# Feed-forward of a two-layer diffusion backbone as one block in three chunks, with rounded down-projection products and a third raw weight slot in the scan

## The reference, cut to what matters

```python
def _conv_ffn(h, lp):
    u, g = jnp.split(h @ lp['ffn_up'], 2, axis=-1)          # 1024 -> 2 * 2816
    g = _dwconv3(g, lp['ffn_conv'], lp['ffn_conv_b'])       # three taps along the tokens
    return (jax.nn.gelu(g, approximate=False) * u) @ lp['ffn_down']   # 2816 -> 1024

# in each layer, after the token mixer; alpha = 4 ** 0.25
x = _layernorm(alpha * x + mod[2] * lat_mix, ln1_g[i], ln1_b[i])
x = _layernorm(alpha * x + mod[5] * _conv_ffn(_modulate(x, mod[3], mod[4]), lp), ln2_g[i], ln2_b[i])
```

## Time and profile before

| | us |
|---|---|
| median of 3 runs | 4132.44 |
| lowest and highest of them | 4118.54, 4132.5 |
| profiled execution, its own time | 4123.52 |
| its span, first to last instruction | 4121.7 |
| TensorE busy in it | 3571.3 (87%) |
| VectorE, ScalarE, GpSimd busy | 1515.8, 997.4, 1047.9 |
| mean granted TensorE clock | 0.942 |

### The profile page before, as it was taken

The page is one execution under the profiler, slowest core; times in us unless marked ns, Lnnn a source line. Parts: engine busy times, 40 slices in busy tenths (PEclk is TensorE's granted clock), DMA queues, the critical chain, the costliest instruction groups (busy, mean ns, idle before and its releaser), DMA issues. The chain is left out here.

```text
span 4121.7 us, 80895 instructions
## 1 busy us (share of the span) xinstructions
PE 3571.3 (87%) x36124; PEld 2659.2 (65%) x36124; DVE 1515.8 (37%) x2207; ACT 997.4 (24%) x1690; POOL 1047.9 (25%) x641
## 2 busy tenths in 40 slices
PE   5979989999787777999899597998889877679987
PEld 4658878888556553888644376877778554448843
DVE  3243434432676244311101524454442663342112
ACT  3312212221464120322100141222121552213200
POOL 2122233333014011322100322243444022224401
PEclk9989999999999889999999798999999999889998
DMA  6653344343214141122243143344443222413321
GB/s 243 205 156 101 105 127 119 91 122 100 93 51 150 69 138 40 57 67 62 94 147 133 51 160 121 94 116 117 132 130 105 100 92 93 163 41 97 87 102 41
DMA packets 454724, 444.30 MB, mean 108 GB/s; under 512 B 19876, under 2 KB 373338, under 8 KB 447466
## 3 DMA queue, kind: packets, MB, share of 16 engines
q1 hardware_dynamic: 452794, 430.35, 33.3%
q10 hardware_dynamic: 1584, 8.78, 0.6%
HBM read 350.32 MB, written 88.74 MB: 107 GB/s over the span
## 5 line engine op out<-in xcount | busy, mean ns | idle before, releaser
L855 PE MATMUL ps<-I-280_h_hi,I-1958_w_hi 128*128 128x256 f32 (+1 forms) x832 | 302.1, 363 | 32.5 <-POOL I-1959_w_lo L329 32.5
L855 PE MATMUL ps<-I-281_h_lo,I-1958_w_hi 128*128 128x256 f32 (+1 forms) x832 | 285.7, 343 | 4.0 <-issue 4.0
L855 PE MATMUL ps<-I-280_h_hi,I-1959_w_lo 128*128 128x256 f32 (+1 forms) x832 | 285.7, 343 | 0.0
L855 PE MATMUL ps<-I-22095_h_hi,I-23492_w_hi 128*128 128x512 f32 (+1 forms) x544 | 216.8, 398 | 32.5 <-POOL I-23493_w_lo L329 30.5
L2074 PE MATMUL ps<-I-21346_w_down,I-18202_hf 128*128 128x512 f32 x528 | 234.1, 600 | 9.1 <-DMA I-21346_w_down<-in_ffn_down 9.1
L855 PE MATMUL ps<-I-22095_h_hi,I-23493_w_lo 128*128 128x512 f32 (+1 forms) x544 | 203.6, 374 | 0.3 <-issue 0.3
L855 PE MATMUL ps<-I-22096_h_lo,I-23492_w_hi 128*128 128x512 f32 (+1 forms) x544 | 203.6, 374 | 0.0
L855 PEld LDWEIGHTS ps<-I-280_h_hi,I-1958_w_hi 128*128 128x128 f32 x832 | 159.3, 192 | 55.5 <-POOL I-1959_w_lo L329 33.7
L2074 PEld LDWEIGHTS ps<-I-21346_w_down,I-18202_hf 128*128 128x128 f32 x528 | 99.2, 191 | 143.3 <-issue 133.3
L338 PE MATMUL ps<-I-18203_h_hi,I-18207_w_hi 128*128 128x512 f32 x704 | 179.7, 336 | 1.1 <-DVE I-18204_h_lo L380 1.1
L338 PE MATMUL ps<-I-18204_h_lo,I-18207_w_hi 128*128 128x512 f32 x704 | 179.5, 336 | 0.0
(11 more groups left out here) (824 smaller groups left out, 8169.3 us busy)
## 6 DMA issues: line engine op xcount, KB each, us to landing
I-1957_w_raw<-in_w_in SPq DMA_DIRECT2D x52, 512.0 KB, 4.7
I-23491_w_raw<-in_w_in SPq DMA_DIRECT2D x52, 512.0 KB, 5.0
I-21350_ada_w<-in_ada_w SPq DMA_DIRECT2D x24, 1024.0 KB, 4.9
I-18206_w_raw<-in_ffn_up SPq DMA_DIRECT2D x44, 512.0 KB, 3.9
I-37126_w_raw<-in_ffn_up SPq DMA_DIRECT2D x44, 512.0 KB, 3.9
proj_d<-I-1960_result SPq DMA_DIRECT2D x52, 384.0 KB, 2.8
I-482_ada_w<-in_ada_w SPq DMA_DIRECT2D x16, 1024.0 KB, 5.7
I-21346_w_down<-in_ffn_down SPq DMA_DIRECT2D x22, 512.0 KB, 5.9
```

The costliest lines, as they stand in the source:

```text
L855: m = pe.matmul(bank(6 + i % 2, n_c), w[:, k, :], hv[:, k, c0:c0 + n_c], start=k == 0 and v == 0, stop=k == KT - 1 and v == 2)
```

## The change

In `rwkv_scan`, the raw ring has three slots, so that the weights of slot s+3 are loaded where those of slot s+2 were. Results go to a DRAM tensor `pair_d` with 272 rows per tile; a q or k tile is stored twice in it, and the swapped copy is fetched in four DMAs of 32 rows instead of eight of 16. `reset` is one tile for both directions, and the swapped copy lands in `ada_row`. `ffn` and `ffn_down` become one `ffn` with one stage: the 22 inner tiles are worked in chunks of 8, 8 and 6, first the up slots of a chunk and then its down slots for either half of the columns. The down weights come through the same rings as the up weights, and the inner tile is split too (`hp`: ScalarE `hf_hi`, GpSimd `hf_lo`), so that down products are three rounded ones. Each of the six passes (chunk, half) ends in VectorE multiplying by the gate row and adding to x. The gate rows are made after up slots 2 and 5, the `ada_w` steps stand behind every second slot from slot 8 on, the final norm goes tile by tile with the normalization on ScalarE, and the output is written by four DMAs, one per tile.

```diff
-            rings = weight_rings(s2, 2, 2)
+            rings = weight_rings(s2, 3, 2)
...
-                        for at_p, from_p in swap:
-                            sp.dma_start(rs[at_p:at_p + 16, :], src[from_p:from_p + 16, 0:SEQ]).then_inc(sem("swap_in"), 16)
+                        for u in range(4):
+                            sp.dma_start(rs[32 * u:32 * u + 32, :], swapped(slots[s][0])[u]).then_inc(sem("swap_in"), 16)
...
-                        if s + 2 < len(slots):
-                            load(s + 2)
+                        if s + 3 < len(slots):
+                            load(s + 3)
...
                         sp.dma_start(proj_d[j, :, 0:w], res[:, s % 2, 0:w]).then_inc(sem(f"stored{s % 2}"), 16)
+                        if s in turned:
+                            sp.dma_start(pair_d[j, TWIN + 16:TWIN + 16 + P, 0:SEQ], res[:, s % 2, 0:SEQ]).then_inc(sem(f"stored{s % 2}"), 16)
...
+        def ffn(l, h, last):
...
+            CH = 8
+            chunks = [range(j, min(j + CH, FT)) for j in range(0, FT, CH)]
...
+            n_pairs = 4 if last else 3
...
+            ada_at = {8 + 2 * e: e for e in range(len(ada))}
...
+                hp = [sb(s2, f"hf_{i}", [P, CH, n_tok], F32R) for i in ("hi", "lo")]
...
+                            pe.wait_ge(sem("hf_lo"), j + 2)
+                            for t in range(nt):
+                                if opens(g) and t % 2 == 0:
+                                    released(first_user[g] + t // 2)
+                                for k in range(2):
+                                    for v, (hv, w) in enumerate(((0, whi), (0, wlo), (1, whi))):
+                                        m = pe.matmul(pt_of(a, t), hp[hv][:, k0 + k, t * P:(t + 1) * P], wide(w)[:, k, :],
+                                                      start=k0 + k == 0 and v == 0, stop=k0 + k == n_k - 1 and v == 2)
...
+                            act.wait_ge(sem("hf"), j + 1)
+                            act.activation(hp[0][:, j % CH, :], cv[:, j % 2, 0:n_tok], ACT.Copy).then_inc(sem("hf_hi"), 1)
...
+                            pool.wait_ge(sem("hf_hi"), j + 1)
+                            pool.tensor_tensor(hp[1][:, j % CH, :], cv[:, j % 2, 0:n_tok], hp[0][:, j % CH, :].bitcast(F32),
+                                               ALU.subtract).then_inc(sem("hf_lo"), 1)
...
+                        dve.tensor_tensor(part[:, i % 2, :], pt_of(cn, t), gate[:, t // LT, c], ALU.mult).then_inc(sem("z1"), 1)
+                        dve.wait_ge(sem("z1"), i + 1)
+                        if cn[0] == 0:
+                            dve.scalar_tensor_tensor(x[:, t, c], x[:, t, c], ALPHA, part[:, i % 2, :], ALU.mult, ALU.add).then_inc(sem("z2"), 1)
+                        else:
+                            dve.wait_ge(sem("z2"), i + 1 - 2 * nt)
+                            dve.tensor_tensor(x[:, t, c], x[:, t, c], part[:, i % 2, :], ALU.add).then_inc(sem("z2"), 1)
+                        if cn[0] == LC:
+                            dve.wait_ge(sem("z2"), i + 1)
+                            dve.bn_stats(st[:, t, cn[1], :], x[:, t, c]).then_inc(sem("st"), 1)
...
-        def ffn_down(l, hf, last):
...
-                                for t in range(nt):
-                                    if n and g == 0:
-                                        pe.wait_ge(sem("z1"), t + 1)
-                                    for k in range(KG):
-                                        m = pe.matmul(bank(t), hf[:, g * KG + k, t * P:(t + 1) * P], ring[:, i % SL, k, :],
-                                                      start=g == 0 and k == 0, stop=g == NG - 1 and k == KG - 1)
...
-                            dve.tensor_scalar(x[:, t, :], x[:, t, :], mv[:, t, 0:1], rs[:, t:t + 1], ALU.subtract, ALU.mult).then_inc(sem("xn"), 1)
+                        act.activation(x[:, t, :], x[:, t, :], ACT.Identity, bias=nb[:, t:t + 1], scale=rs[:, t:t + 1]).then_inc(sem("xn"), 1)
...
+                            sp.dma_start(dst[:, t, :], x[:, t, :]).then_inc(sem("out"), 16)
...
-        with stage(nc) as (block, sem):
-            @block.sync
-            def _(sp):
-                sp.dma_start(out.rearrange("b (t p) d -> p (b t) d", p=P), x[:, 0:LT, :]).then_inc(sem("out"), 16)
-                sp.wait_ge(sem("out"), 16)
```

More of the change, by code:

```diff
@@ L716, in rwkv_scan @@
             turned = [s for s, (j, _, _) in enumerate(slots) if J_Q <= j < N_PROJ]
[L717 removed]
+            stores = [sum(2 if q in turned else 1 for q in range(s % 2, s + 1, 2)) for s in range(len(slots))]
+            swapped = lambda j: pair_d[j, 16:16 + 2 * TWIN].rearrange("(w u z) t -> u w z t", w=2, z=32)[:, :, 0:16, 0:SEQ]
             chunk_of = lambda d, q: q if d == 0 else 1 - q
@@ new lines, in _ @@
+                    for g, (kind, j, i) in enumerate(slots):
+                        if g + 2 < N:
+                            split(g + 2)
+                        if kind == "up" and i == 1:
+                            pool.wait_ge(sem("hf_hi"), j + 1)
+                            pool.tensor_tensor(hp[1][:, j % CH, :], cv[:, j % 2, 0:n_tok], hp[0][:, j % CH, :].bitcast(F32),
+                                               ALU.subtract).then_inc(sem("hf_lo"), 1)
+                    pool.wait_ge(sem("ln_b"), 16)
@@ L2137, in program @@
+                    dve.wait_ge(sem("ln_g"), 16)
+                    gated((LC, 1), 0)
+                    moments(0)
+                    for t in range(nt):
+                        if t + 1 < nt:
+                            gated((LC, 1), t + 1)
+                            moments(t + 1)
+                        reciprocal(t)
+                        if t:
+                            scaled(t - 1)
+                    scaled(nt - 1)
         for l in range(DEPTH):
```

385 lines of the change are left out of this document (217 added, 168 removed).

## The result

The changed kernel took **4034.7 us** as a median of four runs (4030.7 to 4043.79), against 4132.47 for the kernel before in the same session (4118.54 to 4136.84): a ratio of 0.9769, 95% interval 0.9751 to 0.9788. That is some 95 us gained where 149 were predicted, and outside the predicted range, 19 us above its upper end. The profiled execution took 4036.52; its span is 87.0 shorter than that of the earlier trace rows.

A forecast was written before the change was run, and what follows sets the result against it. TensorE was taken to bound every stage. Savings of 77.5 + 36.1 - 5.1 + 5.0 - 2.1 + 10 + 28 = 149.4 us from the profiled 4123.5 gave 3974, moved up by 4 to 3978; range 3954 to 4016.

The forecast's parts named there:

- Part 5: Scans: the third raw slot removes TensorE's waits for `w_lo` except at the start, 28 us off; fewer DMAs cost nothing.
- Rival A: Scans give nothing back: the recurrence chain takes the stall's place or GpSimd stays bound; 4006 us, chance 0.15.
- Part 1: Down products of both layers: three rounded products of 0.2262 us replace a plain float32 one of 0.855; 77.5 us off.
- Rival C: Down products take 0.641 us, three quarters of the plain float32 time, by the skill page's rule; 3961 us, chance 0.05.
- E: Feed-forward down products: rounded ones in this layout are no cheaper than plain ones; 4055 us, chance 0.03.
- D: Short waits among the feed-forward slots drop TensorE to its low clock; up to 4243 us, chance 0.04.
- Part 2: Border between up and down: gaps vanish, 36.1 us off; gate rows 5.1 on; low clock after the gap 5.0 off.
- Part 3: New feed-forward block: splits and additions stay hidden at no cost; the last two `ada_w` steps put 2.1 us on.
- rival B: Feed-forward block: GpSimd's splits and VectorE's additions hold one another up on SBUF's shared side; 4007 us, chance 0.13.
- Part 4: Ends behind the last down matmul: 26.3 us in layer 0, 24.0 in layer 1; 10 us off over both.

The follow-up runs named there:

- fifth kernel: Against the changed kernel, swapped copy read in eight DMAs of 16 rows instead of four of 32, second store kept though unread: 4005.36 us, ratio 0.9691.

## Why the prediction failed, step by step

**Part 5 failed, twice, and it is 47 us of the 54** by which the gain of 95 falls short of the sum of 149. It said of the new reads that "SyncE's queue gets shorter, nobody ahead of TensorE waits for it". The first clause is right of the issue alone (2.5 us for the four in layer 1, where eight took 3.7 to 4.3): each read was carried by two DMA engines, the queue then stood longer for the writes behind them, and I had counted DMAs and not looked at their shape. The second clause is wrong. GpSimd, ahead of TensorE, waits for exactly these rows in all 16 turns of each layer; its waits for them stood in the trace of before, at 28.7 us, and I hadn't read them. Measured: 38 us on, where the step had nothing; 32 of them for the form of the reads, and 6, within the noise, for the second store. The other sentence, that the second store delays the fetch "in front of GpSimd, whose next split has longer than that", assumed a slack that GpSimd, which waits for the plain rows 71.5 us in layer 0, doesn't have.

The third slot was put at 28 off and is worth 19, good to some 15; what shows the failure is that with it alone 24.2 and 21.6 us of TensorE's waits for `w_lo` are left, where the step left 19.0 and 15.4. I had followed the late load of the earlier trace rows back to the inputs in SyncE's queue, which was right, and concluded that an earlier load would cure it. But the queue delays everything behind the block: take the weights away from there and the fetch is next, and GpSimd's order (turn, then split) passes that on to the weights. "Who would be late next is the chain on VectorE and ScalarE": it was not; it was the same queue through another tile. Rival A, which had the right place (scans that give nothing back), had the wrong mechanism and, at 4006, no room for a loss.

**Part 1 came out.** Down products start every 0.2265 us (0.2262 predicted) at a clock of 1.00, with the activations as the stationary side, and 440 of them gave what they should. Rival C, three quarters by the rule on passes, is off: 3 x 0.2265 is 0.68 and not 0.641. E and D fell too; the clock in the blocks is 1.00.

**Part 2 came out**: the two gaps are gone, the gate rows cost 1.7 us a time (their slots took 10.19 and 10.05, their neighbours 8.32 to 8.48), and layer 1's block was met within 0.3.

**Part 3** was mis-sized in layer 0, by 10.0 us with what it left out. "The 24 `ada_w` steps take what they took" is 1.18 each and not 1.04 among rounded products, 3.4 us. "I count nothing but in the range" for the joints was right at every joint but one, and that one cost 4.1. It is rival B, at one joint instead of six, and only together with the statistics: the Trainium skill's rule (SBUF — State Buffer, "Who interferes with whom") showed itself where the page puts it, 2.71 us against 0.69, and TensorE waited for `part` at no other joint. Some 2.5 us of the block are left over and stay open; the three slots with a transpose take 0.4 us more than their neighbours, and whether they did so before I haven't measured. No split was late for `hf_hi` or `hf_lo`.

**Part 4** met 24.0 in layer 1, but by luck, and was half right in layer 0 (28.6 for 26.3). GpSimd began 2.6 us behind the last matmul, as worked out (2.4), but its first four tiles stand 5.5 apart and not 4.3:

```profile
2253.74 2.34 POOL L2156 TENSOR_TENSOR I-49_x<-I-49_x,I-18171_ln_b 128x1024 f32<-128x1024 f32 x1 [15.41 <-DVE I-49_x L2194]
2259.27 2.34 POOL L2156 TENSOR_TENSOR I-49_x<-I-49_x,I-18171_ln_b 128x1024 f32<-128x1024 f32 x1 [3.19 <-DVE I-49_x L2194]
...
2277.39 2.34 POOL L2156 TENSOR_TENSOR I-49_x<-I-49_x,I-18171_ln_b 128x1024 f32<-128x1024 f32 x1 [1.16 <-DVE I-49_x L2194]
```

While VectorE still had sums of later tiles to do, its addition ran beside GpSimd's each time and took 2.33 to 2.40 and not 0.69: a tile was 0.68 + 2.35 + 0.69 + 0.6 of small ones + 1.22 = 5.5 long. I had let this addition and the small instructions behind it run beside GpSimd's. Once VectorE has no more sums to do, the tiles stand 3.5 to 3.6 apart, less than the 4.3. In layer 1 the gaps are 5.5, 3.6 and 3.5, which come to 12.6 for three times 4.3 by two errors that cancel; in layer 0, with three of the long gaps and two of the short, they don't.

**The range** should have had a loss in the scans. The bound that was given there, 0, was "the slot gives nothing"; that the reads could cost something had no bound at all, because they were counted at nothing with a reason instead of a row.

## What to carry to other kernels

Before a late transfer is given a deeper ring, list everything that stands behind the same block on the in-order queue and everyone who waits for it: cutting the block helps all of them (26 us here, with no memory, though not every wait went), a deeper ring helps one and hands the place to the next. Count a DMA by its shape and not by itself: here a read whose source had an outermost dimension of 2 kept two of the 16 DMA engines busy. Merging eight small DMAs into four such ones made the rows come 6 us after the last issue, where they came after 1.4 (fifth kernel), and held up the writes issued behind them. And when a step changes what an engine waits for, read that engine's waits first, also if it is not the bottleneck.

## What was not expected of the hardware

- Four reads of 64 KB from 32 rows in one block: GpSimd waits 7.9 us in 16 turns; from four blocks of 8 rows 41.9; from two of 16 rows 71.5. The share of the DMA engines that they keep busy is 0.13 to 0.14 with two blocks and 0.26 to 0.29 with four, and it stays at 0.14 where all four DMAs have been issued: they did not spread over different engines.
- Writes of 256 KB issued behind such reads landed after 6.8 us with two blocks, 4.4 with four and 2.5 with one.
- A float32 step of 1.04 us costs 1.18 among rounded products when it stands alone, and 1.02 in a pair.
- A wait of TensorE of 2.16 us in a block at the clock 1.00 cost 4.1 in all, since the eight products behind it ran at half the rate.
